# Row scaling on VectorE and a re-ordered token stage in a two-layer decoder trunk

## What is computed

```python
def rms_norm(x, g, eps=NORM_EPS):
    x32 = x.astype(jnp.float32)
    y = x32 * lax.rsqrt(jnp.mean(x32 * x32, axis=-1, keepdims=True) + eps)
    return (y * g.astype(jnp.float32)).astype(x.dtype)
...
def conv_ffn(h, w_gate, w_up, conv_w, conv_b, w_down):
    S = h.shape[1]
    a = h @ w_gate
    ap = jnp.pad(a, ((0, 0), (CONV_WIDTH - 1, 0), (0, 0)))
    conv = conv_b
    for t in range(CONV_WIDTH):
        conv = conv + conv_w[t] * ap[:, t:t + S]
    return (jax.nn.gelu(conv, approximate=True) * (h @ w_up)) @ w_down
```

## Time and profile before

| what | us |
|---|---|
| median of 3 runs | 1426.13 (1422.9 to 1429.44) |
| the profiled execution | 1428.51 |
| its span in the trace | 1426.7 |
| PE busy | 1381.5 (97%) |
| DVE busy | 908.8 (64%) |
| ACT busy | 580.0 (41%) |
| POOL busy | 144.6 (10%) |

### The profile page before, as it was taken

How to read it: one execution, slowest core, us unless ns; L and a number is a source line. 1 busy time by engine, 2 the same in 40 slices (tenths; PEclk the granted TensorE clock), 3 DMA queues, 4 the chain that set the end, 5 groups by cost and what they waited for, 6 DMA issues and landing times.

```text
span 1426.7 us, 18130 instructions
## 1 busy us (share of the span) xinstructions
PE 1381.5 (97%) x7066; PEld 1126.3 (79%) x7066; DVE 908.8 (64%) x1604; ACT 580.0 (41%) x990; POOL 144.6 (10%) x250
## 2 busy tenths in 40 slices
PE   4999999999999999999999999999999999999998
PEld 3779788888788788887888777777888878887886
DVE  7677899885678777764556548887367444443223
ACT  4543344445533334331215537777353333332112
POOL 2001000000311111100112002221120000000000
PEclk9999999999999999999999999999999999999999
DMA  9437434331256555553652132212135333333231
GB/s 333 141 95 218 140 96 141 104 104 45 74 162 193 176 177 178 177 150 127 194 166 69 62 89 60 60 60 74 45 108 173 89 89 103 89 93 99 89 98 65
DMA packets 168666, 171.49 MB, mean 120 GB/s; under 512 B 5269, under 2 KB 140806, under 8 KB 168582
## 3 DMA queue, kind: packets, MB, share of 16 engines
q1 hardware_dynamic: 154224, 119.59, 27.8%
q0 software_dynamic: 13824, 50.34, 10.6%
q10 hardware_dynamic: 534, 0.41, 0.1%
HBM read 168.22 MB, written 2.10 MB: 119 GB/s over the span
## 4 chain that ended last, share of the span: by engine, by line
PE 84%; DVE 7%; ACT 4%; issue 2%; POOL 2%; DMA 1%; SPq 0%; ACTq 0%; DVEq 0%; POOLq 0%
PE ps L634 21%; PE ps L562 15%; PE ps L564 15%; PE ps L563 15%; PE ps L1100 3%; PE ps L809 2%; PE ps L899 2%; ACT prob L1710 2%; PE ps L616 2%; PE ps L887 2%; PE ps L605 2%; PE ps L1218 1%; PE ps L685 1%; DVE prob L2378 1%; POOL osum L2554 1%
## 5 line engine op out<-in xcount | busy, mean ns | idle before, releaser
L562 PE MATMUL ps<-hhi,whi 128*128 128x512 f32 (+1 forms) x1008 | 396.8, 394 | 4.1 <-DVE hlo L1896 3.5
L1821 DVE TENSOR_TENSOR wlo<-raw,whi 128x1024 fp32r<-128x1024 f32 x200 | 244.1, 1221 | 238.6 <-ACT whi L1324 238.6
L564 PE MATMUL ps<-hhi,wlo 128*128 128x512 f32 (+1 forms) x1008 | 388.5, 385 | 0.0
L563 PE MATMUL ps<-hlo,whi 128*128 128x512 f32 (+1 forms) x1008 | 387.9, 385 | 0.0
L1324 ACT ACTIVATE whi<-raw 128x1024 fp32r<-128x1024 f32 x200 | 210.1, 1052 | 256.7 <-PE ps L634 175.7
L562 PEld LDWEIGHTS ps<-hhi,whi 128*128 128x128 f32 x1008 | 189.8, 188 | 47.2 <-issue 7.0
L564 PEld LDWEIGHTS ps<-hhi,wlo 128*128 128x128 f32 x1008 | 189.8, 188 | 41.6
L563 PEld LDWEIGHTS ps<-hlo,whi 128*128 128x128 f32 x1008 | 190.2, 189 | 39.4 <-issue 1.0
L1952 DVE SCALAR_TENSOR_TENSOR macc<-mraw,csil,macc 128x256 f32<-128x256 f32 x294 | 142.4, 484 | 14.4 <-DMA mraw<-in_mod_ffn_w_dram 5.2
L634 PE MATMUL ps<-whi,ghi 128*128 128x512 f32 x352 | 110.7, 395 | 1.7 <-DVE tmp L2316 1.7
L634 PE MATMUL ps<-wlo,ghi 128*128 128x512 f32 x352 | 110.9, 396 | 0.0
(11 more groups left out here) (281 smaller groups left out, 1995.0 us busy)
## 6 DMA issues: line engine op xcount, KB each, us to landing
mraw<-in_mod_ffn_w_dram POOLq DMA_DIRECT2D x48, 512.0 KB, 4.2
raw<-in_ffn_w_gate_dram SPq DMA_DIRECT2D x44, 512.0 KB, 3.8
raw<-in_ffn_w_up_dram SPq DMA_DIRECT2D x44, 512.0 KB, 3.7
raw<-in_ffn_w_down_dram SPq DMA_DIRECT2D x44, 512.0 KB, 3.6
mraw<-in_mod_mix_w_dram POOLq DMA_DIRECT2D x32, 512.0 KB, 3.9
raw<-in_a_w_qkv_dram SPq DMA_DIRECT2D x28, 512.0 KB, 4.6
mstart<-in_mod_mix_w_dram SPq DMA_DIRECT2D x8, 1024.0 KB, 14.4
mraw<-in_kv_mod_w_dram POOLq DMA_DIRECT2D x16, 512.0 KB, 3.8
```

The source lines that it names most:

```text
L562: pe.matmul(out_, whi[:, slot, cols], rhs_hi, start=first, stop=False)
L563: pe.matmul(out_, whi[:, slot, cols], rhs_lo, start=False, stop=False)
L564: return pe.matmul(out_, wlo[:, slot, cols], rhs_hi, start=False, stop=last)
L1821: dve.tensor_tensor(wlo[:, slot, :], raw[:, slot, :], head, ALU.subtract).then_inc(*at.here(lo_ready, ahead))
```

## The change

1. The scaling of `x_tok` rows by the root leaves PE. DVE writes `x_tok` times the root as one 128x1024 instruction (`scaled_x`) into a free part of the stage's buffers (`scaled_tile`), and `turn_x` is 8 plain transposes with `identf`. POOL's diagonal is gone; a signal `x_root` goes from POOL to DVE, and `x_rms` from DVE to PE.
2. Tiles 0 and 1 are taken through both norms first on ACT, DVE and POOL. `turn_x(0)` and `turn_x(1)` stand earlier: in A ahead of the last tile's third product, in F behind the last tile's third-last and second-last products, in B in the middle of tile 2 (behind its product k = 5). In B (`rows_apart`) ACT and DVE finish pair 0 altogether ahead of tile 2 and 3.
3. The last tile's square and gained of B and of the end of the program run in halves of 512, crossed: ACT squares one half while DVE gains the other.
4. The entries start when half of pair 0's features are there (`n_half`). `turn_x(2)` and `turn_x(3)` stand behind the second chunk in A and B, behind the third in F.
5. `keep_warm` is 12 in A, 12 in F and none in B. In F the one-column sums stand behind `turn_x(3)`, and DVE's reading of them between pair 0's and pair 1's work; PE waits for that reading.
6. Stage A's buffers move up, and `ohi` and `olo` lie on the memory of the attention's queries and keys. Therefore `head_of_o(0)` waits for the last pair's scores and stands behind both weight splits; `head_of_o(1)` stands behind an `exp`. DVE's rests are moved likewise.
7. Row 7 of layer 1's output weights has a place of its own (`last_row_b`).

The diff cut to what the text speaks of, with the common indentation of each piece taken off:

```diff
-WARM, WARM_START, WARM_SUMS, WARM_LATE = 24, 8, 12, 10
+WARM, WARM_START, WARM_SUMS = 12, 8, 12
...
-buffers_a = token_buffers("a", 8 * 1024)
+buffers_a = token_buffers("a", 14 * 1024)
...
+def scaled_tile(buffers, t):
+    u, full = buffers
+    if t > 1:
+        return u[:, t - 2, :]
+    return full[:, 1, 4 * t:4 * t + 4, :].rearrange("p k n -> p (k n)")
...
+hi, lo = h
+for half in range(2):
+    cols = slice(2 * P * half, 2 * P * half + 2 * P)
+    for b in range(3):
+        if half == 0:
             pe.wait_ge(*at.done(lo_ready, b))
-        last = norms > 1 and b == 2 and h == 1
-        mm = half(b, h, 0, DT - 1 if last else DT)
-        if h == 0 and n == 0:
-            turn_x(2)
-            turn_x(3)
-        if h == 1 and not last:
+        for k in range(DT):
+            if b == 0 and k == 0:
+                pe.wait_ge(*at.done(n_half, half))
+            if b == 0 and k == DT // 2:
+                pe.wait_ge(*at.done(n_ready, half))
+            mm = product(banks[b][:, cols], (slots[b], slice(k * P, (k + 1) * P)), hi(k)[:, cols], lo(k)[:, cols],
+                         k == 0, k == DT - 1)
+        if half == 0 and b == 1:
+            turn_x(2, buffers)
+            turn_x(3, buffers)
...
+src = scaled_tile(buffers, t)
 pe.wait_ge(*at.done(u_ready, t | 1))
+pe.wait_ge(*at.done(y_summed, t | 1))
 pe.wait_ge(*at.done(x_rms, t))
 for k in range(DT):
     col = (k % 2) * 2 * P + (t % 2) * P
-    ins = pe.matmul(ps[:, banks[k // 2], col:col + P], x_tok[:, t, tile_cols(k)], rdiag[:, t, :],
-                    start=True, stop=True)
+    ins = pe.transpose(ps[:, banks[k // 2], col:col + P], src[:, tile_cols(k)], identf[:])
...
-if b == 1 and norms:
-    turn_x(0)
+if b < 2 and norms:
+    turn_x(b, buffers_ffn, 2)
...
-if late_sums is None:
-    keep_warm(WARM, ps[:, 4, :])
-else:
-    keep_warm(WARM_LATE, ps[:, 4, :])
-    pe.wait_ge(*at.done(u_ready, 3))
-    late_sums()
+keep_warm(WARM, ps[:, 4, :])
...
-if k == PAIRS - 1:
-    turn_x(0)
+if k == PAIRS - 2:
+    turn_x(0, buffers_a)
+    turn_x(1, buffers_a)
 products(3, k).then_inc(*at.here(chunk_used, k))
...
 at.passed("chunk", PAIRS)
-turn_x(1)
...
-def ffn(pairs, norms):
+    for j, sum_ in enumerate([macc[:, j, :] for j in range(4)] + [macc_late[:, j, :] for j in range(2 * PAIRS_LATE - 4)]):
+        ins = pe.matmul(ps[:, 3, j:j + 1], sum_, onesf[:, 0:1], start=True, stop=True)
+    ins.then_inc(*at.here(late_ready))
...
-pe.wait_ge(*at.done(n_ready, 0))
 for c in range(3):
     pe.wait_ge(*at.done(lo_ready, c))
+    if c == 0:
+        pe.wait_ge(*at.done(n_half, 0))
+    if c == 2:
+        pe.wait_ge(*at.done(n_ready, 0))
     values_b(0, c, (0, 1))
-    if c == 1:
-        pe.wait_ge(*at.done(full_front, 1))
-        pe.wait_ge(*at.done(full_back, 1))
-        pe.wait_ge(*at.done(t_free, -1))
-        turn_x(2, 2)
-        turn_x(3, 2)
-pe.wait_ge(*at.done(n_ready, 2))
+pe.wait_ge(*at.done(full_front, 1))
+pe.wait_ge(*at.done(full_back, 1))
+turn_x(2, buffers_ffn, 2)
+turn_x(3, buffers_ffn, 2)
+late_columns()
+pe.wait_ge(*at.done(late_read))
 for c in range(3):
+    if c == 0:
+        pe.wait_ge(*at.done(n_half, 2))
+    if c == 2:
+        pe.wait_ge(*at.done(n_ready, 2))
     values_b(0, c, (2, 3)).then_inc(*at.here(chunk_used, c))
...
+    if k == HEADS_B - 3:
+        turn_x(0, buffers_b)
+        turn_x(1, buffers_b)
 mm.then_inc(*at.here(y_done))
 at.passed("ydone")
 for k in range(2, HEADS_B):
-    if k == HEADS_B - 1:
-        turn_x(0)
     products(3, k).then_inc(*at.here(chunk_used, k))
 at.passed("chunk", HEADS_B)
-turn_x(1)
-pe.wait_ge(*at.done(u_ready, 2))
-keep_warm(WARM, ps[:, 4, :])
...
+if rows_apart:
+    fronts(0, norms[0])
+    heads(0, norms[0])
+    square_y(2)
+    square_x(2)
+    for _ in range(3):
+        split_next()
+    square_last_y()
+    square_x(3)
+elif len(norms) > 1:
...
+act.wait_ge(*at.done(ps_ready, 3))
 head_of_o(0)
-chunk()
-head_of_o(1)
-chunk()
 at.passed("tjob")
 read_prob(0)
 exp(3, 0)
+head_of_o(1)
...
+def gained_last():
+    first, second = slice(0, T), slice(T, 2 * T)
+    dve.wait_ge(*at.done(chunk_used, 2 - split[0]))
+    dve.wait_ge(*at.done(x_new, NT - 3))
+    dve.tensor_tensor(u[:, 1, second], ps[:, 7, :], gb[:, second], ALU.mult).then_inc(*at.here(u_half))
+    dve.wait_ge(*at.done(y_half))
+    dve.tensor_tensor(u[:, 1, first], ps[:, 6, :], gb[:, first], ALU.mult).then_inc(*at.here(u_ready, NT - 1))
...
+def scaled_x(t):
+    dve.wait_ge(*at.done(x_root, t))
+    dve.tensor_scalar(scaled_tile(buffers, t), x_tok[:, t, :], X_RMS[:, t:t + 1], None, ALU.mult).then_inc(*at.here(x_rms, t))
...
 gained(0)
 added(0)
 gained(1)
 added(1)
-gained(2)
-added(2)
-split_next()
-gained(3)
-backs(0, norms[0])
-if len(norms) > 1:
+scaled_x(0)
+scaled_x(1)
+if rows_apart:
+    backs(0, norms[0])
     rests(0, norms[0])
+    gained(2)
+    added(2)
+    for _ in range(3):
+        split_next()
+    scaled_x(2)
+    gained_last()
     added(3)
-    late_read()
+    scaled_x(3)
+elif len(norms) > 1:
+    gained(2)
     split_next()
-    backs(0, norms[1])
-    split_next()
-    rests(0, norms[1])
-else:
-    added(3)
+    backs(0, norms[0])
     rests(0, norms[0])
     split_next()
+    added(2)
+    gained(3)
+    split_next()
+    added(3)
+    scaled_x(2)
+    backs(0, norms[1])
+    scaled_x(3)
+    rests(0, norms[1])
+    dve.wait_ge(*at.done(late_ready))
+    dve.tensor_tensor(modc[:, FFN[1]:FFN[1] + 2 * PAIRS_LATE], ps[:, 3, 0:2 * PAIRS_LATE],
+                      bcol[:, FFN[1]:FFN[1] + 2 * PAIRS_LATE], ALU.add).then_inc(*at.here(late_read))
+else:
+    gained(2)
+    added(2)
+    split_next()
+    backs(0, norms[0])
+    rests(0, norms[0])
+    gained(3)
+    added(3)
+    split_next()
+    scaled_x(2)
+    scaled_x(3)
     split_next()
...
 def of_x(t):
     pool.wait_ge(*at.done(x_summed, t))
-    chain(rms(X_RMS, X_SUM, slice(t, t + 1)))
-    pool.tensor_scalar(rdiag[:, t, :], identf[:], X_RMS[:, t:t + 1], None, ALU.mult).then_inc(*at.here(x_rms, t))
-for t in range(NT):
-    of_y(t)
-    if norms:
-        of_x(t)
+    rms(X_RMS, X_SUM, slice(t, t + 1)).then_inc(*at.here(x_root, t))
...
+FIRST, SECOND = [(0, 0), (0, 1), (1, 0), (1, 1)], [(0, 2), (0, 3), (1, 2), (1, 3)]
+APART = [(0, 2), (1, 2), (0, 3), (1, 3)]
```

More of the change, by code:

```diff
@@ L397, in yoco_trunk @@
         GROUPS = ((0, 1), (2,), (3,))
-        V_BANKS = (4, 7, 2, 3)
+        V_BANKS = (4, 5, 2, 3)
         def turned_banks(pair, norms):
-            return (0, 1, 5, 6) if pair and norms == 2 else range(4 * pair, 4 * pair + 4)
+            return (0, 1, 6, 7) if pair and norms == 2 else range(4 * pair, 4 * pair + 4)
         def score_banks(head, group):
@@ L415, in row_of_b @@
                 return whi[:, slots[k], :], wlo[:, slots[k], :]
-            a, j = ((khi, klo), 2 * (k - 3)) if k < 7 else ((hhi, hlo), 0)
-            return tuple(part[:, j:j + 2, :].rearrange("p a n -> p (a n)") for part in a)
+            if k == 7:
+                return last_row_b[:, 0, :], last_row_b[:, 1, :]
+            j = 2 * (k - 3)
+            return tuple(part[:, j:j + 2, :].rearrange("p a n -> p (a n)") for part in (khi, klo))
         def value_cols(g):
@@ L636, in row_products, with enter @@
                 return mm
-            def enter(sources, order):
-                norms = len(set(order))
+            def enter(h, buffers):
                 banks, slots = [], []
@@ L669, in enter @@
                             mm.then_inc(*at.here(chunk_used, b))
-                if norms > 1:
-                    half(2, 1, DT - 1, DT).then_inc(*at.here(chunk_used, 2))
-                at.passed("norm", 2 * norms)
+                at.passed("norm", 2)
                 at.passed("tok", NT)
@@ L1147, in enter_b @@
                 part_of_b(0, 1)
+                for b in (-1, -2):
+                    pe.wait_ge(*at.done(t_free, b))
                 for c in range(DT // 2):
@@ L1902, in token_stage @@
                 if not norms:
-                    for t in range(NT):
+                    for t in range(NT - 1):
                         gained(t)
                         added(t)
+                    gained_last()
+                    added(NT - 1)
                 else:
@@ L2555, in _ @@
                 at.passed("unit1")
-            token_stage(True)
+            token_stage(True, True, FIRST + APART)
+            pool.wait_ge(*at.done(x_turned, -1))
             ffn(1)
-            token_stage(False)
+            token_stage(False, True, [(0, t) for t in range(NT)])
 _INS = ['x', 'c', 'positions', 'mod_mix_w', 'mod_mix_b', 'mod_ffn_w', 'mod_ffn_b',
```

154 lines of the change are left out of this document (84 added, 70 removed).

## The result

The changed kernel took 1407.46 us (median of 4 runs, 1405.64 to 1411.16) against 1427.58 for the kernel before beside it: 20.1 us less, a ratio of 0.9867 (95% interval 0.9834 to 0.9900). The forecast was 1419.0, its range ended at 1413.5. The profiled execution took 1408.34 with a span of 1406.3, against 1426.7.

What follows compares the result with a forecast made beforehand. PE was taken as the bound, so only PE work outside the result and PE's waits could pay. −2.1 (last attention pair) + 5.0 (A) + 0.4 (F) + 3.7 (B) = 7.0 off 1426.13: 1419.1, said as 1419.0; range 1413.5 to 1425.

Steps and rivals of the forecast that it cites:

- A: Token stage with norms at the first ConvFFN's entry: second half of the tokens starts at 387.25, not 392.26, 5.0 us gained.
- F: Token stage with norms at the second layer's entry: 3.2 us gained, less 2.8 for half clock, net 0.4.
- B: Token stage with norms at the second ConvFFN's entry: 5.0 us gained, less 1.3 for the clock, net 3.7.
- last attention pair: Row products ahead of A wait for later `olo` writes, +0.75 and +1.35: 2.1 us lost.
- second half: In each stage, when the second half of the tokens starts on PE: 5.0, 3.2 and 5.0 us earlier.
- the clock's charge: In B, possible half clock after a 3.5 us wait between transposes: 1.3 us charged, ends 0 and 3.4.
- PE's wait in A for `wlo`: New wait at A's second chunk, as `wlo` stands on DVE behind the third and fourth tile's additions: 1.8 us.
- A turn by transposes: Turning one tile by eight plain transposes with `identf` in each stage with norms: 0.78 us, where 1.8 was needed.
- Rival (a): The clock holds in F and B, without the 2.8 and 1.3 us charged: 1414.9 us, chance 0.15.
- rival (c): Half clock at every new wait, six in all, 3.4 us a drop: 1429.2 with three more; chance 0.08.
- The rule on transposes: Transposes don't count as busy PE for the clock; two drops in A and B, 1425.8 us, chance 0.04.
- The reason given for B: Pair 0, turned in the third tile's products, is ready 5 us before the last tile ends; PE enters at 1032.5.

Runs made afterwards that it cites:

- before_32: The kernel before with `stat` one word wider, moving every buffer behind it by 32 bytes, no instruction changed: 1415.85 us against 1426.19, ratio 0.9925.
- after_unshifted: The changed kernel with the extra `stat` word put into a free column of `small`, so all addresses are those of the kernel before: 1416.51 us, ratio 0.9927.
- after_fill_b: The changed kernel with 12 keep-warm matmuls in stage B between the turns of tiles 2 and 3: 1405.75 us, ratio 0.9848.
- after_b_as_a: The changed kernel with stage B written as stage A: pair 0 turned later, last tile not in halves, no warming in B: 1408.17 us, ratio 0.9871.
- after_no_half: The changed kernel with entries waiting for all of a pair's features (`n_ready`), not half (`n_half`): 1411.53 us, ratio 0.9900.

## Why the prediction was wrong

**The step that failed.** The prediction says that only two things can pay here, PE work that is no part of the result and the places where PE stands still. Its sum thus costs each edit by the instructions it adds, removes and moves, and has no term for the matmuls that stay: their price was taken as fixed, without a reason. The word added to `stat` changed it. That was 10 us (before_32: 10.3, with 7.8 to 13.7 by its interval), more than the 7.0 of the whole sum.

Where it lies is read from after_unshifted against the changed kernel, which have the same instructions and 10.2 us between their spans. The two down products give 4.6 of it, gate and up 0.7 in FFN 0 and 1.2 in FFN 1, everything up to the last attention pair 1.4. Another 1.7 is the clock's: after_unshifted has 3.4 us of half clock from about 976, between F and B, and the changed kernel none. The remainder is under 1 us and wasn't split further.

**The stages went as worked out.** The differences outside them shift all that follows, so each time worked out for the forecast (B's second half without the clock's charge) is moved here by the table's difference ahead of it.

| | forecast, moved | measured |
|---|---|---|
| A, entry | 373.6 - 1.2 = 372.4 | 372.25 |
| A, second half | 387.25 - 1.2 = 386.1 | 385.65 |
| F, entry | 772.0 - 9.1 = 762.9 | 762.62 |
| F, second half | 791.2 - 9.1 = 782.1 | 782.11 |
| B, entry | 1032.5 - 12.45 = 1020.0 | 1020.03 |
| B, second half | 1047.9 - 12.45 = 1035.4 | 1035.85 |

PE's wait in A for `wlo` was 1.19 (forecast 1.8), in B ahead of the last turn 2.93 (3.5), in F 3.30 (3.7). The last attention pair cost 1.83 (2.1), with the second wait as the larger one, as said, at 1.16. A turn by transposes took 0.96 (0.78).

**The clock.** In F the half clock came: it fell at about 777 and returned at about 787, so 5 us of it lay behind the restart (5.7 forecast). In B it lasted 3.4 us (1029.5 to 1033) and not 6.8, and the second half came 0.45 us behind the time worked out without it, where 1.3 was charged. The ends of that term held. Rival (a), the clock holds, was wrong in this profile; rival (c), a fall at every new wait, too: there was none in A (waits of 1.2 and 1.6 us), and it wouldn't have made the kernel slower than before. The rule on transposes that the prediction weighs there from the Trainium skill (page "TensorE: Matmul & The Clock Gate", section "Part 4: PE-mode transpose") can't be judged: both falls have a wait beside the turns or sums, and after_fill_b keeps the clock at 1.00 with the same transposes.

**Size.** after_unshifted has the addresses of the kernel before, so the steps between these two price the edits alone (its starts at the places of the first table: 309.76, 342.09, 387.49, 736.24, 810.53, 1007.39 and 1042.52):

| | forecast | measured at equal addresses |
|---|---|---|
| last attention pair | +2.1 | +2.07 |
| A | -5.0 | -5.25 |
| F | -0.4 | -0.54 |
| B | -3.7 | -5.15 |
| sum | -7.0 | -8.87 |

In between, from A to F, from F to B and behind B, the two differ by 0.2 us or less a step. So all but one term were sized right; B's 5.15 is the 5.0 that was worked out ahead of the 1.3 us charged for the clock. In the changed kernel F's step of 1.18 holds the shift's part in the end of the down product and in the value products, too. Edits and shift come to about 17.4 us by rows (8.9, and 10.2 less the 1.7 of the clock); with the 3.4 us in which the two profiled executions differ by their clock this is the span's 20.4 within half a us. The medians' 20.1 has an interval from 14.3 to 23.7.

One more slip stands in the range: its low end is said to be the clock held and the last attention pair free of cost, which by the forecast's own numbers is 1414.9 - 2.1 = 1412.8 and not 1413.5. The measured 1407.46 is below either.

**The reason given for B** was wrong although its number was near. The prediction took the early turn of pair 0 as the point of B; after_b_as_a shows that the second half waits for the last tile's chain in either form. What B gains should then come from the turns' shorter time, the warming left out, and the entry by halves; of these only the last was tried alone (after_no_half).

## What to carry over

A change can move addresses without touching an instruction; compare the placement of the operands as well as the order, and read the start-to-start time of long unbroken runs of matmuls in both traces first. Where PE is 96% busy, try the distance between the weight operand and the streamed operand modulo 256 bytes: here 96 bytes of padding gave 29 us (2.0%), more than a rewrite of three stages. Before a step between two profiles is put down to an edit, look at the granted clock in both: here the two profiles differ by 3.4 of their 20.4 us in that alone. Finishing a part early pays only if the part that comes last doesn't wait for something else.
